# Scaling second-table rows on ScalarE and summing them by accumulating transposes

## What is computed

```
v1, i1 = lax.top_k(s1, 16); v2, i2 = lax.top_k(s2, 16)
sc, pos = lax.top_k(sums of v1 and v2, 16);  idx = experts at pos
g = softmax(sc)
act = gelu(einsum('thkd,td->thk', u[idx], t), approximate=False)
out = einsum('thk,thkd->td', g * act, v[idx])
x = rmsnorm(x + out)
```

## Time and profile before

| | us |
|---|---|
| median of 3 runs | 2814.39 |
| the runs | 2812.92, 2814.39, 2819.12 |
| span of the profiled execution | 2813.7 |
| busy in it: PE, PEld | 2636.0, 1852.2 |
| busy in it: DVE, ACT, POOL | 1755.5, 1010.2, 966.4 |

### The profile page before, as it was taken

The page is one execution under the profiler, slowest core; times in us unless marked ns, Lnnn a source line. Parts: engine busy times, 40 slices in busy tenths (PEclk is TensorE's granted clock), DMA queues, the critical chain, the costliest instruction groups (busy, mean ns, idle before and its releaser), DMA issues.

```text
span 2813.7 us, 32400 instructions
## 1 busy us (share of the span) xinstructions
PE 2636.0 (94%) x12469; PEld 1852.2 (66%) x12469; DVE 1755.5 (62%) x2445; ACT 1010.2 (36%) x1667; POOL 966.4 (34%) x731
## 2 busy tenths in 40 slices
PE   8999999999999999999999799998988989899986
PEld 7877898888888888778789455555543434333432
DVE  4767564555456555567647787677657875455466
ACT  5567565544677454445553121111110000000011
POOL 6013151000000000441101654666556767355464
PEclk9999999999999999999999899999999999999998
DMA  7544403455445546434455999999999999999998
GB/s 239 183 145 146 144 16 136 163 205 188 156 141 177 175 133 215 145 120 150 135 180 196 368 404 404 410 405 411 413 407 391 396 398 410 416 398 412 414 410 328
DMA packets 209641, 751.53 MB, mean 267 GB/s; under 512 B 25133, under 2 KB 29449, under 8 KB 150857
## 3 DMA queue, kind: packets, MB, share of 16 engines
q0 software_dynamic: 74400, 475.38, 41.9%
q1 hardware_dynamic: 135088, 274.09, 28.4%
HBM read 809.09 MB, written 2.10 MB: 288 GB/s over the span
## 4 chain that ended last, share of the span: by engine, by line
DMA 25%; PE 24%; DVE 7%; POOL 5%; issue 5%; ACT 1%; POOLq 0%; DVEq 0%; ACTq 0%
PE bank L2223 24%; DMA UROW<-in_peer_u_dram,WORK 20%; DMA VROW<-in_peer_v_dram,WORK 5%; DVE BIG L2162 3%; POOL UROW L668 2%; POOL VROW L676 2%; DVE BIG L1721 0%; DVE WL L1421 0%; DMA UROW<-in_peer_v_dram,WORK 0%; DVE BIG L2117 0%; DVE UROW L2162 0%; PE bank L2359 0%; ACT WH L796 0%; PE bank L2785 0%; PE bank L2401 0%
## 5 line engine op out<-in xcount | busy, mean ns | idle before, releaser
L2223 PE MATMUL bank<-VROW,WORK 128*128 128x512 f32 x1864 | 863.6, 610 | 124.5 <-DMA VROW<-in_peer_v_dram,WORK 102.6
L2162 DVE CUSTOM_DVE_ANT_0 BIG<-UROW,BIG 128x2048 f32<-128x2048 f32 x252 | 578.3, 2295 | 398.9 <-DMA UROW<-in_peer_u_dram,WORK 383.6
L2223 PE MATMUL bank<-HX,WH 128*128 128x512 f32 (+1 forms) x2784 | 760.0, 345 | 12.0 <-issue 4.8
L2223 PEld LDWEIGHTS bank<-VROW,WORK 128*128 128x128 f32 x1864 | 353.1, 195 | 578.2 <-issue 534.8
L2223 PE MATMUL bank<-HX,WL 128*128 128x256 f32 x2128 | 596.7, 280 | 0.0
L2223 PEld LDWEIGHTS bank<-HX,WH 128*128 128x128 f32 x2784 | 480.5, 189 | 84.4 <-issue 16.9
L668 POOL DMA_INDIRECT UROW<-in_peer_u_dram,WORK x256 | 340.7, 1331 | 557.8 <-DVE WORK L2162 323.6
L1427 DVE TENSOR_TENSOR WL<-RAW,WH 128x1024 fp32r<-128x1024 f32 (+2 forms) x261 | 305.1, 1180 | 297.4 <-ACT WH L796 296.6
L2223 PE MATMUL bank<-WH,HX 128*128 128x512 f32 (+1 forms) x1472 | 452.1, 390 | 3.5 <-ACT BIG L739 2.5
L676 POOL DMA_INDIRECT VROW<-in_peer_v_dram,WORK x252 | 396.5, 1573 | 112.2 <-issue 76.3
L2223 PEld LDWEIGHTS bank<-HX,WL 128*128 128x128 f32 x2128 | 402.9, 189 | 0.1
(11 more groups left out here) (386 smaller groups left out, 2393.3 us busy)
## 6 DMA issues: line engine op xcount, KB each, us to landing
RAW<-in_w_in_odd_dram SPq DMA_DIRECT2D x64, 1024.0 KB, 5.4
RAW<-in_w_in_even_dram SPq DMA_DIRECT2D x48, 1024.0 KB, 5.2
RAW<-in_w_in_dram SPq DMA_DIRECT2D x44, 1024.0 KB, 5.1
RAW<-in_w_out_even_dram SPq DMA_DIRECT2D x16, 1024.0 KB, 5.0
RAW<-in_w_out_odd_dram SPq DMA_DIRECT2D x16, 1024.0 KB, 5.1
RAW<-in_w_out_dram SPq DMA_DIRECT2D x16, 1024.0 KB, 5.2
RAW<-in_peer_wq_dram SPq DMA_DIRECT2D x16, 1024.0 KB, 5.1
DROW<-in_peer_u_dram SPq DMA_DIRECT2D x32, 512.0 KB, 7.8
```

The lines of the kernel that those rows point to most:

```text
L2162: dve.tensor_tensor_reduce(out=product, in0=UROW[:, b, :], in1=TT[m], op0=ALU.mult, op1=ALU.add, scale=1.0, scalar=0.0, accum_out=DOT[:, n ...
L2223: return pe.matmul(dst, lhsT, rhs, start=start, stop=stop, skip_group_check=True)
```

## The change

For all rows up to 243 ACT no longer makes a diagonal: it waits until the v row has landed and scales it in place, each partition (token) by its coefficient. PE then takes the scaled row in 16 pieces of 128x128 as weights against the identity, with the transpose flag, and lets the turned pieces add up in banks 0 to 3 over the rows. So the banks hold the sums turned, with tokens along the columns. At the end of block 0 ACT copies the banks to WIDE (`sums_out`, ahead of row 128), and PE turns them back, four transposes beside each of the rows 128, 130, 132 and 134 (`turn_back`); DVE adds the four results one at a time behind the dots of rows 139, 141, 143 and 145. Block 1 is turned back at row 244, into banks 4 to 7, and rows from 244 on are added there by diagonals as before. The dense second-table steps of block 1 add to the turned sums, so each of their 512-column matmuls becomes four of 128 columns with the operands exchanged. The 17 rows up to 243 that DVE added itself go to ACT and PE. SP's load of the last norm's weights now waits for the fourth add of block 0, since WIDE lies in the place that it loads into. The four semaphores of an earlier load become two.

```diff
-ADD_AT = PICKS + 8
+ADD_AT = PICKS + 11
...
-ON_DVE = tuple(v for v in range(60, 108) if v % 8 == 7) + tuple(v for v in range(160, N_PICKS - 8) if v % 8 == 7)\
-    + (N_PICKS - 7, N_PICKS - 5, N_PICKS - 4, N_PICKS - 2)
+ON_DVE = (N_PICKS - 7, N_PICKS - 5, N_PICKS - 4, N_PICKS - 2)
+TURNED = N_PICKS - 12
+BACK_AT = tuple(PICKS + 2 * g for g in range(4))
...
-                        sp.dma_start(dst[:, :, 0:32], src[:, 4 * j:4 * j + 4, 2560:2592]).then_inc(s[f"w_gate{j}"], 16)
+                        sp.dma_start(dst[:, :, 0:32], src[:, 4 * j:4 * j + 4, 2560:2592]).then_inc(s[f"w_gate{j // 2}"], 16)
...
-                    sp.wait_ge(s["u_dot"], PICKS)
+                    sp.wait_ge(s["o_add"], 4)
...
+            def sums_out(m):
+                act.wait_ge(s["v_used"], rows_before(ON_PE, TURNED if m else PICKS))
+                if m:
+                    act.wait_ge(s["d_v"], V_STEPS)
+                for j in range(4):
+                    act.activation(WIDE[m][:, j * NW:(j + 1) * NW], bank[j], ACT.Copy).then_inc(s["w_out"], 1)
             def diagonals(q):
                 act.wait_ge(s["p_coef"], q + 1)
                 for n in range(BATCH * q, BATCH * (q + 1)):
-                    if n not in ON_DVE:
+                    if n == PICKS:
+                        sums_out(0)
+                    if n < TURNED and n not in ON_DVE:
+                        act.wait_ge(s[v_landed(n)[0]], v_landed(n)[1])
+                        act.activation(v_buffer(n), v_buffer(n), ACT.Copy, scale=COEF[:, n:n + 1])\
+                            .then_inc(s["p_diag"], 1)
+                    elif n not in ON_DVE:
                         k = rows_before(ON_PE, n)
-                        if k >= 4:
+                        if n >= TURNED + 4:
                             act.wait_ge(s["v_used"], k - 3)
                         act.activation(DIAG[:, k % 4, :], ID[:, :], ACT.Copy, scale=COEF[:, n:n + 1])\
                             .then_inc(s["p_diag"], 1)
+                    if n == TURNED:
+                        sums_out(1)
                     beside_row(n)
...
-            def add_outputs():
-                dve.wait_ge(s["v_used"], rows_before(ON_PE, PICKS))
-                for j in range(4):
-                    x = XR[:, 0, j * NW:(j + 1) * NW]
-                    dve.tensor_tensor(x, x, bank[j], ALU.add).then_inc(s["o_add"], 1)
+            def add_outputs(j):
+                dve.wait_ge(s["w_t"], j + 1)
+                x = XR[:, 0, j * NW:(j + 1) * NW]
+                dve.tensor_tensor(x, x, bank[4 + j % 2], ALU.add).then_inc(s["o_add"], 1)
...
-                if n == ADD_AT:
-                    add_outputs()
+                j = step_at(n, ADD_AT, 2, 4)
+                if j is not None:
+                    add_outputs(j)
...
-                for m in range(MT):
-                    ins = mm(bank[4 * (1 - m) + c], ACTED[j // 8][:, j % 8, m * P:(m + 1) * P], DROW[:, c // 2, cs],
-                             m == 0 and j == 0, m == 0 and j == DENSE - 1)
+                mm(bank[4 + c], ACTED[j // 8][:, j % 8, 0:P], DROW[:, c // 2, cs], j == 0, j == DENSE - 1)
+                for q in range(4):
+                    ins = mm(bank[c][:, q * P:(q + 1) * P], DROW[:, c // 2, (c % 2) * NW + q * P:(c % 2) * NW + (q + 1) * P],
+                             ACTED[j // 8][:, j % 8, P:T], False, False)
                 ins.then_inc(s["d_v"], 1)
+            def turn_back(m, g):
+                pe.wait_ge(s["w_out"], 4 * m + g + 1)
+                if m == 0 and g >= 2:
+                    pe.wait_ge(s["o_add"], g - 1)
+                for q in range(4):
+                    c0 = g * NW + q * P
+                    ins = pe.matmul(bank[4 + (g if m else g % 2)][:, q * P:(q + 1) * P], WIDE[m][:, c0:c0 + P], ID[:, :],
+                                    start=m == 0 and q == 0, stop=False, is_transpose=True, skip_group_check=True)
+                ins.then_inc(s["w_t"], 1)
             def beside_row(v):
@@ -2853,15 +2885,29 @@
                     continue
                 k = rows_before(ON_PE, n)
                 m, pick = n // PICKS, n % PICKS
-                if pick == 0 and m == 1:
-                    pe.wait_ge(s["o_add"], 4)
+                if n == PICKS:
+                    pe.wait_ge(s["w_out"], 4)
+                if n == TURNED:
+                    pe.wait_ge(s["o_add"], 8)
                 pe.wait_ge(s["p_diag"], k + 1)
-                pe.wait_ge(s[v_landed(n)[0]], v_landed(n)[1])
-                for j in range(2 if n == SHARED else 4):
-                    ins = mm(bank[j], DIAG[:, k % 4, :], v_buffer(n)[:, j * NW:(j + 1) * NW], pick == 0,
-                             pick == PICKS - 1 or (n == SHARED - 1 and j >= 2))
+                if n < TURNED:
+                    for c in range(KT):
+                        ins = pe.matmul(bank[c // 4][:, c % 4 * P:(c % 4 + 1) * P], v_buffer(n)[:, c * P:(c + 1) * P], ID[:, :],
+                                        start=pick == 0 and c % 4 == 0, stop=False, is_transpose=True, skip_group_check=True)
+                else:
+                    pe.wait_ge(s[v_landed(n)[0]], v_landed(n)[1])
+                    for j in range(2 if n == SHARED else 4):
+                        ins = mm(bank[4 + j], DIAG[:, k % 4, :], v_buffer(n)[:, j * NW:(j + 1) * NW], n == TURNED,
+                                 n == (SHARED if j < 2 else SHARED - 1))
                 ins.then_inc(s["v_used"], 1)
+                if n in BACK_AT:
+                    turn_back(0, BACK_AT.index(n))
+                if n == TURNED:
+                    for g in range(4):
+                        turn_back(1, g)
                 beside_row(n)
```

More of the change, by code:

```diff
@@ L310, in two_blocks @@
             const_in ln_first vec_in masks vec_t cols_set x_in out_done eps_set act_chain dve_chain pool_chain
-            w_full0 w_full1 w_full2 w_full3 w_gate0 w_gate1 w_gate2 w_gate3 g_t r_of r_v r_c r_hi r_lo r_one wh_done wl_done ws_used tile_free half_left low_out
+            w_full0 w_full1 w_full2 w_full3 w_gate0 w_gate1 g_t r_of r_v r_c r_hi r_lo r_one wh_done wl_done ws_used tile_free half_left low_out
             n_rstd n_root n_sq n_sum n_x n_t n_xt n_h n_l r_diag r_row r_set t_scaled y_ready y_h y_l
@@ L322, in two_blocks @@
             u_dot p_gelu p_coef p_diag v_used v_on o_add
+            w_out w_t
             tt_set d_row0 d_row1 d_t d_tc d_m d_act d_v g_in g_g g_mix
@@ L400, in two_blocks @@
         G_REST = BIG[:, 13, 768:1024]
+        WIDE = [BIG[:, 0:2, :].rearrange("p a b -> p (a b)"), BIG[:, 10:12, :].rearrange("p a b -> p (a b)")]
         DONE = [BIG[:, 12:14, :].rearrange("p a b -> p (a b)"), BIG[:, 10:12, :].rearrange("p a b -> p (a b)")]
@@ L788, in split @@
                         if r["kind"] == "gate":
-                            act.wait_ge(s[f"w_gate{sub // 2}"], 16)
+                            act.wait_ge(s[f"w_gate{sub // 4}"], 32)
                     if r["base"] > 0 or not first or sub >= 4:
@@ L2209, in _ @@
                 x = XR[:, 1, j * NW:(j + 1) * NW]
-                dve.tensor_tensor(x, x, bank[j], ALU.add).then_inc(s["o_add"], 1)
+                dve.tensor_tensor(x, x, bank[4 + j], ALU.add).then_inc(s["o_add"], 1)
             root(1)
```

## The result

The changed kernel takes 2835.85 us (median of 4 runs, 2835.17 to 2837.70) against 2815.14 us for the kernel before, run beside it: a ratio of 1.0074, interval 1.0060 to 1.0089. It is **slower by 21 us**. The forecast was 2816.8 us and no change, the range ended at 2828: the measured time lies 8 us beyond it.

The account below looks back on a forecast made before the run. The prediction took transfers to bound the expert stage and all else as hidden: 2813.7 us of span plus 2.4 for the turned gates is 2816.1, and 0.7 for runs over span gives 2816.8 us, range 2806.5 to 2828.

Parts of the forecast that it names:

- The bound: Expert layer from about 1590 us on: transfers bound the stage, with DMA share 1.00 and 1.01.
- PE and ACT: Gathered rows: 16 transposes at 1.9 us replace 3.60 us on PE, ACT scales in 2.0 us; both covered by transfers.
- The border of the token blocks: Between blocks 0 and 1: four single DVE adds replace one piece; gain between 0 and 1.1 us, taken as 0.
- the dense steps: Block 1's second-table steps: four 128-column matmuls cost 1.0 to 2.0 times one of 512, under a microsecond more, covered.
- The new wait: Scaling on ACT needs the landed row, so ACT work behind it waits and delays DVE and POOL; +2.4 us in all.
- two kinds of it feed DVE: Of ACT's work behind scalings, only block 0's gate exponentials and the turned-gate copies feed DVE; 0 and +2.4 us.
- (a): Three gate exponentials of block 0 behind the scalings of rows 15, 23 and 31: hidden, 0 us, with 1.8 us margin.
- the slot: At the first exponential, the delayed row is usable at 1657.6, before its turn at 1659.4, 3.5 pairs behind row 15.
- R1: Rival, slower: the queue does not carry the three exponentials, 3 x 3.3 = 9.9 us on top, 2826.7 us; chance 0.24.
- (b): Three ACT copies of the turned gates behind row 111's scaling: DVE goes on 2.4 us later, nothing hides it, +2.4 us.
- R2: Rival, far slower: row transposes at half clock (2990 us) or as two-pass matmuls (+37 to beyond 400 us); chance 0.04.
- R3: Rival, faster: relieving PE and DVE lengthens the queue and closes holes in the DMA share, 2807.5 us; chance 0.14.

Follow-up runs that it names:

- the three moves: Changed kernel with gate exponentials one row group earlier, turned-gate copies ahead of row 111's scaling, squares ahead of the scalings of rows 232 to 235: 2819.11 us, ratio 1.0011.

## Why the prediction was wrong, point by point

- **The bound**: right. DMA share 1.01 in both kernels between the holes, and PE relieved of half its row work changes nothing.
- **PE and ACT**: right in kind, near in size. 2.37 us a row of transposes where 1.9 was taken (1.7 to 2.4 given), 2.00 us a scaling where 2.0 was taken. Both covered. (Of the 17 rows that DVE gave up, 16 lie up to row 243; row 247 went to PE by a diagonal.)
- **The border of the token blocks, the dense steps**: no loss there clear of the scatter; by the bytes the changed kernel is 8.3 us behind at 240 MB, 7.5 at 260 and 9.2 at 280, and the distance stays within 1 us from there to 460 MB. The price of a dense step, given as 1.0 to 2.0 times, was 1.0: at 2658 us two passes of 512 columns took 1.02 us and eight of 128 took 1.05.
- **The new wait**: the mechanism was named, and it is what costs. Two steps of its sum failed.
  - *"two kinds of it feed DVE"*: there are three. The squares of block 0 stand behind the scaling of row 235, and DVE's sum of them behind the dot of row 241. This step was left out, and it is the largest term: 10 us. The prediction's last sentence names just this kind of gap, "a copy of ACT that I have not followed to its waiter", and it should have been closed ahead of the sum: DVE waits for several semaphores of ACT between the dots, and only two were followed. It could have been priced in the trace of before: there DVE's sum began at 2719.16, behind the dot of row 241, and row 235 landed at 2727.97 (issued at 2713.17, 14.8 us to landing), 8.8 us later. With 2.0 for the scaling and 3.0 for the four squares, that makes 13.8 us, which is the wait that came.
  - *(a), "hidden, 0"*: 6 us. At the first of the three, DVE and POOL came as worked out, to 0.6 us; the last step, the slot, was wrong, in its number (7.95 us joins the issue of one row to the use of another) and as a test. Both are told below the list. Rival R1 had the place and the mechanism, and put 3.3 us on each; all three together cost 6, and by the bytes moved the first cost some 4 of it.
  - *(b), +2.4*: DVE's wait grew from 0.73 to 3.03 us, 2.3, as forecast. The link was only half named: the copies stand behind row 111, but PE's turn stands behind row 110 just as late, so moving the copies alone gave nothing. In the bytes the place costs 1.8 us, with about 1 us of scatter from one stretch to the next; in the time no run shows it clear of the noise.
- **R2**: half of it is seen, and no cost of it. The granted clock does fall, and rows then take 3.0 to 3.7 us, but that is under the pace of the rows. (Its 4.53 us for 20 transposes at 8.27 us stand ahead of the first clock record of that trace, at 13.4 us; that they ran at half clock is borne out by 3.59 us for 16 at a granted 0.50 in the changed kernel.)
- **R3**: refuted for PE by the run with half of its row work; with the three moves DVE is relieved of its rows too, and the kernel is not faster.

The number in (a): the dot at 2135.78 in the earlier trace rows is not that of the row issued at 2127.83. That row takes the buffer of the dot that ended just before, at 2127.04, and the rows in the three other buffers stand ahead of it (dots at 2127.18, 2133.14 and 2135.78). Its own dot came 12.4 us behind the issue, not 7.95. Here is that dot in the timeline, and under it the time from issue to landing of this one row:

```profile
2140.22 2.29 DVE L2162 CUSTOM_DVE_ANT_0 BIG<-UROW,BIG 128x2048 f32<-128x2048 f32 x1 [2.14 <-DMA UROW<-in_peer_u_dram,WORK]
...
DMA to landing us min/median/max: 12.4/12.4/12.4
```

With 12.4 the forecast's own test gives 1649.6 + 12.4 = 1662.0 against the slot at 1659.4: late, not hidden, and over the 9.8 us at which R1 decides. There was no margin of 1.8 us.

The test in (a): I asked when the late row's own turn would come. In the changed kernel the row issued at 1649.08 took 11.2 us and landed at 1660.2; before, issued at 1643.11, it took 17.0 and landed at 1660.1. So it met its turn, and time was lost all the same, because the queue thins out before it is empty: the share began to fall about 5 us behind the last issue, when the median row would still have been 12 us from its landing. The trace holds sixteen updates of the semaphore for a row, as many as there are DMA engines; for this row before, they run from 5 to 17 us behind its issue. If each is one engine's, the quickest engines had only some 5 us of work queued and stood idle while the slowest still landed rows on time. No run tests that reading.

Nor were the three the same "by construction": DVE waited 7.1, 5.5 and 3.6 us, and POOL paused 10.7 us from issue to issue at the first, 8.8 at the second and under 6 at the third. And a pause has no one price: over the 35 us from the last issue on, the share was 0.99 with the pause of 8.8 us, 0.94 with 10.7, 0.88 with 9.5 at the turned gates and 0.75 with 14.6 at the squares; in the kernel before it was 0.97 with 7.0 and 0.92 with 7.4 at the turned gates.

The sum with the terms as measured: 10 for the squares and 6 for the exponentials, shown in the time, and some 2 for the turned gates, seen in the bytes alone and not shown in the time, make 18 of 20.7 us; the three moves together gave back 17.7.

## What to carry to other kernels

When an edit makes an in-order engine wait for data where it used to wait for an early small thing, list every semaphore that this engine raises behind the new wait, and follow each to its waiter, to the end of the loop: the cost is not in the engine, it is in who stands behind it. If the stage is bound by transfers, price such a stall by the pause it makes in the issues, with the share that went missing behind pauses of like length in like places, and not by one row's latency. Where a latency is used, count the buffers to make sure that the use belongs to the issue. And an engine that is 97% busy may still be hidden: leave half of its work out and look at the time before you make it lighter.

## What the runs showed of the hardware

TensorE's granted clock fell in stretches where PE had idle time between its pieces of work, without an effect on the time that these runs can show: the kernel before with half of PE's row work ran at a mean of 0.935, where it is 0.985 with all of it, and took the same time. From 2660 us on in the changed kernel, with the dense steps between the rows, and then from 2700 us on without them:

```profile
2660.00:2680.00 20.00, 14.87 (x104) 12.20 (x104) 9.28 (x9) 8.23 (x6) 10.08 (x9) 1.00 1.02 417
2680.00:2700.00 20.00, 13.12 (x94) 10.88 (x94) 9.28 (x9) 8.85 (x6) 7.99 (x9) 1.00 1.02 417
2700.00:2720.00 20.00, 13.65 (x78) 12.35 (x79) 12.71 (x14) 8.23 (x6) 10.86 (x10) 0.74 1.01 392
2720.00:2740.00 20.00, 10.77 (x68) 9.42 (x66) 5.84 (x7) 9.62 (x6) 11.17 (x7) 0.83 1.00 413
```

At 1.00 (2.4 GHz) a row of 16 transposes takes 1.97 us; where the clock falls, some rows take twice that:

```profile
2695.52 1.97 PE L2898 MATMUL bank<-ID,VROW 128*128 128x128 f32 x16 [0.89 <-ACT VROW L1332]
2700.18 3.59 PE L2898 MATMUL bank<-ID,VROW 128*128 128x128 f32 x16 [2.69 <-ACT VROW L1332]
2705.11 1.97 PE L2898 MATMUL bank<-ID,VROW 128*128 128x128 f32 x16 [1.34 <-ACT VROW L1332]
```

Here it fell when PE had only these rows with gaps of 1 to 3 us between them, and came back in between; at 1600 to 1700 us (0.86) it also fell with dense steps between the rows. The kernel before with half of PE's row work, which has no transposes in its rows, shows the same: 0.67 and 0.76 in the 40 us from 2700, with gaps of 0.6 to 6 us. The Trainium skill, "TensorE: Matmul & The Clock Gate", Part 4: PE-mode transpose, says that the full-speed state does not engage for transposes. These rows don't bear that out for fp32 transposes: single rows of nothing but transposes ran at full speed after others at half, and plain matmuls with as much idle time lost the clock as well.

Sixteen accumulating fp32 transposes cost PE about half of what the four plain fp32 matmuls of 512 columns cost that move the same data (1.97 against 3.60 us at full clock), with a scaling of 2.00 us on ACT ahead of them.
